# An encoder layer step on one core: the up projection takes its weight chunks in pairs, two accumulator banks in turn

## The reference

```python
mix = (g_ssm * y_ssm + g_mla * y_mla) @ lp['w_out']
h = _layernorm(ALPHA * x + mix, lp['ln1_g'], lp['ln1_b'])
ff = jnp.square(jax.nn.relu(h @ lp['w_up'])) @ lp['w_down']
y = _layernorm(ALPHA * h + ff, lp['ln2_g'], lp['ln2_b'])
```

## Time and profile before

| | |
|---|---|
| median of 3 timed runs | 806.37 us (805.86 to 807.22) |
| the profiled execution | 805.36 us, its span 803.5 us |
| TensorE busy | 789.1 us, 98% |
| VectorE busy | 589.3 us, 73% |
| ScalarE busy | 479.1 us, 60% |
| HBM traffic | 163 GB/s over the span |
| TensorE's clock | full in all slices but the last |

### The profile page before, as it was taken

How to read it: one execution, slowest core, us unless ns; L and a number is a source line. 1 busy time by engine, 2 the same in 40 slices (tenths; PEclk the granted TensorE clock), 3 DMA queues, 4 the chain that set the end, 5 groups by cost and what they waited for, 6 DMA issues and landing times.

```text
span 803.5 us, 15403 instructions
## 1 busy us (share of the span) xinstructions
PE 789.1 (98%) x6191; PEld 760.1 (95%) x6191; DVE 589.3 (73%) x972; ACT 479.1 (60%) x839; POOL 93.3 (12%) x192
## 2 busy tenths in 40 slices
PE   9999999999999999999999999999999999999993
PEld 7999999999899899999999999999999999999993
DVE  5997956846755768989988997866698887655444
ACT  5793854855665578666565664443557887533332
POOL 0225112022013001111000100000000000001222
PEclk9999999999999999999999999999999999999997
DMA  8559356246346335555455544655555555555531
GB/s 309 170 173 362 108 160 209 80 158 196 109 128 187 125 125 177 157 181 164 140 177 179 170 144 144 216 163 178 159 156 159 160 160 171 166 157 163 178 106 59
DMA packets 37432, 132.25 MB, mean 165 GB/s; under 512 B 4705, under 2 KB 5361, under 8 KB 37105
## 3 DMA queue, kind: packets, MB, share of 16 engines
q1 hardware_dynamic: 30960, 109.49, 43.2%
q0 software_dynamic: 5632, 19.93, 7.7%
q10 hardware_dynamic: 768, 1.84, 0.6%
HBM read 127.17 MB, written 4.08 MB: 163 GB/s over the span
## 4 chain that ended last, share of the span: by engine, by line
PE 97%; DMA 1%; DVE 1%; ACT 1%; ACTq 0%; issue 0%; DVEq 0%
PE ps_acc L441 19%; PE ps_acc L442 18%; PE ps_acc L443 18%; PE ps_row L442 3%; PE ps_row L443 3%; PE ps_row L441 3%; PE ps_cb L442 2%; PE ps_tr L442 2%; PE ps_tr L443 2%; PE ps_cb L443 2%; PE ps_tr L441 2%; PE ps_cb L441 2%; PE ps_row L767 1%; PE ps_acc L565 1%; PE ps_tr L735 1%; PE ps_ss L627 1%
## 5 line engine op out<-in xcount | busy, mean ns | idle before, releaser
L1323 DVE TENSOR_TENSOR wlo<-wraw,whi 128x1024 fp32r<-128x1024 f32 x203 | 247.4, 1224 | 137.0 <-ACT whi L923 136.4
L923 ACT CAST whi<-wraw 128x1024 fp32r<-128x1024 f32 x203 | 212.1, 1046 | 135.2 <-DMA wraw<-in_wst 134.4
L441 PE MATMUL ps_acc<-xh,whi 128*128 128x288 f32 x560 | 171.0, 305 | 0.0
L442 PE MATMUL ps_acc<-xl,whi 128*128 128x288 f32 x560 | 165.2, 295 | 0.0
L443 PE MATMUL ps_acc<-xh,wlo 128*128 128x288 f32 x560 | 165.1, 295 | 0.0
L441 PEld LDWEIGHTS ps_acc<-xh,whi 128*128 128x128 f32 x560 | 105.3, 188 | 8.0 <-issue 7.2
L442 PEld LDWEIGHTS ps_acc<-xl,whi 128*128 128x128 f32 x560 | 105.4, 188 | 0.5
L443 PEld LDWEIGHTS ps_acc<-xh,wlo 128*128 128x128 f32 x560 | 105.3, 188 | 0.0
L1378 DVE SCALAR_TENSOR_TENSOR cv<-xp,vec,cv 128x292 f32<-128x292 f32 x96 | 50.1, 522 | 16.5 <-ACT cv L985 14.2
L441 PE MATMUL ps_acc<-o_h,whi 128*128 128x288 f32 x128 | 39.1, 305 | 0.0
L442 PE MATMUL ps_acc<-o_l,whi 128*128 128x288 f32 x128 | 37.8, 295 | 0.0
(11 more groups left out here) (454 smaller groups left out, 2288.9 us busy)
## 6 DMA issues: line engine op xcount, KB each, us to landing
wraw<-in_wst SPq DMA_DIRECT2D x203, 512.0 KB, 3.5
rows<-rows_p POOLq DMA_DIRECT2D x8, 512.0 KB, 4.4
v_raw<-in_wst POOLq DMA_DIRECT2D x8, 512.0 KB, 5.3
side<-in_ukT POOLq DMA_DIRECT2D x8, 256.0 KB, 3.9
side_v<-in_ukT POOLq DMA_DIRECT2D x8, 256.0 KB, 3.6
out_ssm<-s_out POOLq DMA_DIRECT2D x8, 256.0 KB, 2.6
x<-in_xT ACTq DMA_DIRECT2D x4, 288.0 KB, 4.7
ax<-in_xT POOLq DMA_DIRECT2D x1, 1152.0 KB, 7.2
```

The costliest lines, as they stand in the source:

```text
L441: pe.matmul(out, w, mh, start=first, stop=False)
L442: pe.matmul(out, w, ml, start=False, stop=False)
L923: act.copy(whi[:, s % RING, :], wraw[:, s % RING, :]).then_inc(split_hi, 1)
L1323: tt(wlo[:, s % RING, :], wraw[:, s % RING, :], whi[:, s % RING, :].bitcast(F32), ALU.subtract).then_inc(split_lo, 1)
```

## The change

The function `up(b)` becomes `up_pair(b)` and runs for b = 0, 2, ..., 30. It waits for both chunks' `split_lo`, and for the bank of the second of them (`u_evac` at least b + 1 - 5, where up(b) waited for b - 5). Then the three passes of each k are written out, each for both chunks before the next pass. Both `chunk_used` counts are raised at the last k. `if b == 2` stands in the loop as before, which now is behind chunks 2 and 3. ScalarE, VectorE, GpSimd and SyncE have the programs of before.

```diff
-            def up(b):
-                wait_split(("u", b))
+            def up_pair(b):
+                pair = (b, b + 1)
+                for c in pair:
+                    wait_split(("u", c))
                 if b >= UB:
-                    pe.wait_ge(u_evac, b - UB + 1)
+                    pe.wait_ge(u_evac, b + 1 - UB + 1)
                 elif b >= 4:
                     wait_evac(pe, ("o", 6))
                     wait_evac(pe, ("o", 7))
-                out = up_banks[b % UB]
                 for k in range(KB):
                     if b == 0:
                         pe.wait_ge(e_lo, k + 1)
-                    mm = passes(out[:, 0:E], *part(("u", b), k), e_h[:, k, :], e_l[:, k, :], k == 0, k == 7)
-                mm.then_inc(chunk_used, 1)
+                    for c in pair:
+                        pe.matmul(up_banks[c % UB][:, 0:E], part(("u", c), k)[0], e_h[:, k, :], start=k == 0, stop=False)
+                    for c in pair:
+                        pe.matmul(up_banks[c % UB][:, 0:E], part(("u", c), k)[0], e_l[:, k, :], start=False, stop=False)
+                    for c in pair:
+                        mm = pe.matmul(up_banks[c % UB][:, 0:E], part(("u", c), k)[1], e_h[:, k, :],
+                                       start=False, stop=k == KB - 1)
+                        if k == KB - 1:
+                            mm.then_inc(chunk_used, 1)
 
             pe.wait_ge(gb_lo, 2)
-            for b in range(FB):
-                up(b)
+            for b in range(0, FB, 2):
+                up_pair(b)
                 if b == 2:
```

## The result

| | median | range | runs |
|---|---|---|---|
| before | 806.12 us | 804.96 to 807.22 | 4 |
| changed | 812.12 us | 811.77 to 812.49 | 4 |

The ratio is 1.0074, with a 95% interval of 1.0062 to 1.0086: slower by 6 us. The forecast was 811.8. A ratio is worked out from all runs of both kernels and differs from that of the medians by up to 0.0005.

A forecast was written before the change was run, and what follows sets the result against it. TensorE, busy 98% of the span, was taken to bound the kernel. Stalls of 1.6 + 0.8 + 2.8 = 5.2 us plus 0.2 refill made 5.4, giving 810.8 profiled and 811.8 us forecast; 8-in-10 range 807 to 817.

The forecast's parts named there:

- T: Up stage: the end of a pair of chunks, when both its ring slots come free together.
- the four pairs that were named: Up stage: TensorE stalls at pairs 6, 10, 14 and 22, 0.8 to 1.6 us each; chance 0.75.
- A clock below 1.00 behind a stall: TensorE's granted clock: a value below 1.00, the 2.4 GHz level, behind the stalls was listed as showing the forecast wrong.
- Place 1: Pair (6, 7): later LayerNorm sums delay ScalarE's `wb` of chunk 1 to 604.4; stall 1.6 us.
- Place 2: Pairs (8, 9), (10, 11), (12, 13): ScalarE's `wb` behind two casts, 0.78 us late; only pair 10 pays, 0.8 us.
- Place 3: Pairs (14, 15) and (22, 23): VectorE does ff_low before the chunk's subtraction; 1.4 us at each, 2.8 in all.
- the credit: Pairs 8 to 12: a stall just taken counts for the next pair, so pairs 8 and 12 pass without waiting.
- The refill: TensorE refilling its pipe after a stall: between 0 and 0.1 us each, 0.2 us added for four.
- (b): Up-stage passes: same-bank accumulation makes them 134.5 ns and alternation frees it; 10.5 us back, net 804.3 us; chance 0.08.
- (a): Ring too tight everywhere: first of two loads lands with the second, 1.3 later; 11.5 us more, 817.9; chance 0.12.
- (c): Whole kernel: nothing measurable, the stalls fall in overlooked spare time; 806.4 us; chance 0.05.

The follow-up runs named there:

- The first two experiments: Changed kernel with chunk-by-chunk passes and slot freeing, keeping pair waits and late sums: 807.42 us; kernel before with both slots freed at the odd chunk's end: 805.92 us.
- the run with a load of 3.6: Changed kernel, with VectorE's subtraction ahead of the second ff_low in loops 12 and 20: 809.78 us, ratio 1.0047.
- the run with the waits alone: Changed kernel with passes chunk by chunk and each slot freed at its chunk's end; pair waits and late sums kept: 807.42 us, ratio 1.0022.
- the kernel with the sums inside: Changed kernel with the two LayerNorm sums inside pair (2, 3), ahead of its k = 4: 812.91 us, and again 811.55 us.

## Why the prediction was right

**The mechanism.** Joint freeing moves the start of the chain of load, cast and subtraction to T, and the pair's wait moves its end to T + 6.46. The first two experiments show that neither end alone makes the waits at 10, 14 and 22; the one at 6 comes with the pair's wait and the late sums alone. The waits came at the four pairs that were named, for the engines that were named. A clock below 1.00 behind a stall had been called a sign of being wrong: the first profile has none, the second has one behind the longest wait (last section).

**The terms.** The prediction's stalls are delays of a start, counted from when the next pass would have started (602.87 at pair 6). The profile's idle time begins 0.16 later, so 0.16 has to be added to compare.

| wait at pair | predicted | idle measured | delay of the start |
|---|---|---|---|
| 6 | 1.6 | 1.52 | 1.68 |
| 10 | 0.8 | 1.48 | 1.64 |
| 14 | 1.4 | 1.32 | 1.47 |
| 22 | 1.4 | 1.06 | 1.22 |
| sum | 5.2 | 5.4 | 6.0 |

Place 1: the chain came out (`wb` of chunk 1 ends at 604.76, less the 0.4 by which the stage starts later 604.36, where 604.4 was predicted), and the wait is 1.5 idle too where nothing is freed jointly. Place 2: the chain was right in its steps, but in the changed kernel's two profiles its load took 4.2 and 5.1 us, where I had taken 3.5. It also left out the 0.14 us from the end of the copy (619.38) to TensorE's start (619.52). In the run with a load of 3.6 the delay is 0.98, and 0.78 + 0.1 + 0.14 is 1.02. Place 3: the two waits went with VectorE's order alone; why the one at 22 is the shorter in the first profile (1.06, and 1.25 in the second) is not worked out. Pairs 8 and 12 did not wait in either profile of the changed kernel, as the credit has it; no run took the credit away.

**The term that was mis-sized** is the stall at pair 10, 0.8 for 1.64, by its load above all. The refill was put at 0.2 for four. Counted in the same way it is 0.08 each, 0.3 in all, inside the bound of 0.1 each. Delays of 6.0, refills of 0.3 and 0.1 at pair 20 make the 6.4 us of the stage, where I had 5.4. That the idle times sum to 5.4, close to the predicted 5.2, is luck in part: they leave out 0.16 each, and pair 10 is longer and pair 22 shorter than worked out. The median moved by 6.0 where I had said 5.4, and load times differ from one execution to the next. The sum of rival (b) comes to -2.2 by its terms, not -2.1; nothing hangs on it.

**The rivals.** (a), a ring too tight everywhere, is refuted as put: the first of two loads is not slowed by the second (3.5 at 603.29). It is right in a weaker form. With 0.55 to spare a load over 4.0 us shows: in the first profile that of chunk 21 took 4.02, and pair 20 came 0.1 late. (b), a gain by alternation, is refuted by the equal counts of passes. The Trainium skill ("TensorE: Matmul & The Clock Gate", Back-to-back issue gap) gives 123.3 ns at 290 columns for an isolated warm matmul; in this stream, with a new weight load for each pass, 134 ns was measured, and that stands. (c), nothing measurable, is refuted by the interval.

## What to carry to other kernels

Before two steps are joined, write down for each resource when it is given back and when it is wanted next, and move both ends: a ring with 7 us to spare was left with 0.55, and what that spare time had hidden (a wait for another engine ahead of the subtraction, two casts ahead of the copy that frees a bank) became the end of the path. By the working, a stall is credit for the step behind it, so a shortage at every pair may show at every second one. And spare time in a ring pays for late transfers too, which an average never shows.

## What was not expected of the hardware

**Late loads came with an instruction fetch in flight.** In the changed kernel a stretch with punctual loads, 603.2 to 608.5, has only the loads' queue (packets, MB, share):

```profile
q1 hardware_dynamic: 288, 1.05, 59.3%
```

The stretch of the late pair of loads, 611.4 to 617.6, has one packet more, on a queue for instructions:

```profile
q1 hardware_dynamic: 288, 1.05, 55.7%
q8 instruction: 1, 0.02, 1.1%
```

By the share this packet holds one DMA engine of 16 for 1.1 us. In the profiles of the changed kernel and its variants each first load of a pair that took 4.1 us or more had such a packet within its flight, and so had the two slowest loads (4.1 and 4.2) of the run with the waits alone, whose loads go out one by one. The reverse does not hold: the run with 0.8 at pair 10 had one at the start of its load, which took 3.6, and in the kernel before fifteen loads of the stage had such a packet in flight and took 3.4 to 3.9. So this is found together, not shown as a cause, and no edit tested it. In eight profiles of the changed kernel and its variants such a packet, starting between 610.6 and 614.9, is in flight with the load of chunk 11; if it is the cause, it explains why the loss at pair 10 came again.

**A wait of 2.3 us was once followed by the lower clock.** In the second profile of the changed kernel TensorE's windows behind the wait at pair 10 (busy, matmuls, granted clock, DMA):

```profile
617.00:620.00 3.00, 1.11 (x9) 1.00 0.28 51
620.00:622.00 2.00, 1.59 (x9) 0.82 1.00 412
622.00:624.00 2.00, 2.00 (x10) 0.50 0.11 43
624.00:626.00 2.00, 2.00 (x14) 0.82 0.00 0
626.00:660.00 34.00, 32.67 (x243) 1.00 0.44 154
```

A granted clock of 0.50 is the 1.2 GHz level. Passes started 0.24 us apart in place of 0.134, for some 14 passes, 1.5 us lost on top of the 2.3. Ahead of the wait TensorE had been busy without a gap since pair 6. A wait of 2.4 us in the kernel with the sums inside, at the same pair, left the clock at 1.00. So such a wait can cost more than its length, and it need not. It is part of why this execution was the slowest at 814.73 us.
